# One long convolution in a two-block transformer kernel: running sums in a PSUM bank, three channel tiles for GpSimd

## The reference, cut to what matters

```python
def _mixer(x, mem, ...):
    h = _rmsnorm(x, norm_mix_g)
    proj = h @ w_in
    p_a, p_b, q, p_g = jnp.split(proj, IN_SPLITS, axis=-1)
    gb, gc, v = jnp.split(p_a, 3, axis=-1)
    y_a = (gb * _causal_dwconv(gc * v, conv_a_w)) @ w_a_out        # 3 taps
    u, ug = jnp.split(p_b, 2, axis=-1)
    u = u * jax.nn.sigmoid(ug)
    u = _causal_dwconv(u, conv_b_w) + conv_b_bias                  # 31 taps, per channel
    u = jax.nn.silu(_layernorm(u, ln_b_g, ln_b_b))
    y_b = u @ w_b_out
    k, vm = jnp.split(_rmsnorm(mem, norm_mem_g) @ w_kv, 2, axis=-1)
    ...                                                            # attention of q over k, vm
    g = jax.nn.sigmoid(p_g + b_gate)
    return (g[0] * y_a + g[1] * y_b + g[2] * y_c) @ w_o
```

## Time and profile before

| | |
|---|---|
| time, median of 3 runs | 1298.03 us (1295.3 to 1300.07) |
| the profiled execution's time | 1297.04 us |
| its span in the trace | 1294.9 us |
| TensorE busy | 1199.2 us, 93% of the span |
| VectorE busy | 877.6 us, 68% |
| GpSimd busy | 375.7 us, 29% |

### The profile page before, as it was taken

How to read it: one execution, slowest core, us unless ns; L and a number is a source line. 1 busy time by engine, 2 the same in 40 slices (tenths; PEclk the granted TensorE clock), 3 DMA queues, 4 the chain that set the end, 5 groups by cost and what they waited for, 6 DMA issues and landing times.

```text
span 1294.9 us, 20581 instructions
## 1 busy us (share of the span) xinstructions
PE 1199.2 (93%) x8047; PEld 1110.5 (86%) x8047; DVE 877.6 (68%) x1114; ACT 619.6 (48%) x824; POOL 375.7 (29%) x312
## 2 busy tenths in 40 slices
PE   4999889999899999999867889999999988999997
PEld 4999789999799899999766779999989777999996
DVE  3677998988466688888768846555565485555554
ACT  5554324344453454554657645444453474544442
POOL 1009999801300312222212414880010130100000
PEclk9999999999799999999978799999999979999999
DMA  8453445565226555554343028655555502555550
GB/s 268 162 179 131 146 139 183 165 195 190 70 98 189 164 183 176 190 193 164 113 139 130 1 66 235 195 195 184 179 164 190 193 1 71 188 180 182 193 192 35
DMA packets 139427, 201.01 MB, mean 155 GB/s; under 512 B 3252, under 2 KB 119988, under 8 KB 139372
## 3 DMA queue, kind: packets, MB, share of 16 engines
q1 hardware_dynamic: 138128, 195.83, 46.1%
q0 software_dynamic: 912, 3.17, 1.0%
q10 hardware_dynamic: 332, 1.25, 0.3%
HBM read 199.20 MB, written 1.05 MB: 155 GB/s over the span
## 4 chain that ended last, share of the span: by engine, by line
PE 76%; DVE 16%; ACT 5%; issue 2%; POOL 1%; DMA 1%; POOLq 0%; ACTq 0%; SPq 0%; DVEq 0%
PE ps L1456 70%; DVE wlo L896 4%; DVE work L1039 4%; PE ps L1555 4%; ACT whi L511 2%; PE ps L1591 1%; DVE work L996 1%; DVE work L1091 1%; ACT p_hi L531 1%; DMA x<-in_x 1%; POOL q_lo L395 1%; DVE stat L986 1%; DVE work L1206 0%; DVE stat L983 0%; DVE misc L976 0%
## 5 line engine op out<-in xcount | busy, mean ns | idle before, releaser
L896 DVE TENSOR_TENSOR wlo<-raw,whi 128x2048 fp32r<-128x2048 f32 x174 | 405.4, 2333 | 216.4 <-ACT whi L511 216.3
L511 ACT ACTIVATE whi<-raw 128x2048 fp32r<-128x2048 f32 x189 | 361.0, 1915 | 277.3 <-PE ps L1456 272.2
L1456 PE MATMUL ps<-p_hi,whi 128*128 128x256 f32 x1632 | 466.5, 286 | 23.3 <-DVE wlo L896 18.6
L1456 PE MATMUL ps<-p_lo,whi 128*128 128x256 f32 x1632 | 464.9, 285 | 0.0
L1456 PE MATMUL ps<-p_hi,wlo 128*128 128x256 f32 x1632 | 464.7, 285 | 0.0
L1456 PEld LDWEIGHTS ps<-p_hi,whi 128*128 128x128 f32 x1632 | 316.2, 194 | 28.2 <-DVE wlo L896 12.4
L1456 PEld LDWEIGHTS ps<-p_lo,whi 128*128 128x128 f32 x1632 | 316.4, 194 | 1.5
L1456 PEld LDWEIGHTS ps<-p_hi,wlo 128*128 128x128 f32 x1632 | 316.3, 194 | 0.0
L1456 PE MATMUL ps<-whi,q_hi 128*128 128x512 f32 x376 | 147.3, 392 | 3.5 <-DVE wlo L896 2.0
L401 POOL TENSOR_TENSOR wlo<-raw,whi 128x2048 fp32r<-128x2048 f32 x15 | 69.5, 4637 | 276.9 <-ACT whi L511 276.9
L1456 PE MATMUL ps<-whi,q_lo 128*128 128x512 f32 x376 | 146.8, 390 | 0.0
(11 more groups left out here) (229 smaller groups left out, 1672.7 us busy)
## 6 DMA issues: line engine op xcount, KB each, us to landing
raw<-in_w_in SPq DMA_DIRECT2D x36, 1024.0 KB, 5.0
raw<-in_w_up SPq DMA_DIRECT2D x22, 1024.0 KB, 5.1
raw<-in_up_a SPq DMA_DIRECT2D x16, 1024.0 KB, 5.5
raw<-in_down_a SPq DMA_DIRECT2D x16, 1024.0 KB, 4.9
raw<-in_up_b SPq DMA_DIRECT2D x16, 1024.0 KB, 5.4
raw<-in_down_b SPq DMA_DIRECT2D x16, 1024.0 KB, 4.9
raw<-in_od_w_qkv SPq DMA_DIRECT2D x12, 1024.0 KB, 5.2
raw<-in_w_down SPq DMA_DIRECT2D x11, 1024.0 KB, 5.0
```

What stands on the lines that cost most here:

```text
L511: nc.scalar.activation(whi[:, g % R, :], raw[:, g % R, :], ACT.Copy).then_inc(hi_ready, 1)
L896: nc.vector.tensor_tensor(wlo[:, g % R, :], raw[:, g % R, :], whi[:, g % R, :].bitcast(F32), ALU.subtract).then_inc(lo_ready[g % R], 1)
L1456: ins = nc.tensor.matmul(dst, lhs, rhs, start=first and n == 0, stop=last and n == 2)
```

## The change

- The running sums of the long convolution on VectorE are the two halves of PSUM bank 7. The taps read `misc` and the weights in `vec` where they lie, so the copies are gone. The last odd tap writes into `conv`, and the last addition reads the even sum from the bank and this one from `conv`.
- GpSimd takes tiles 0, 2 and 4 in place of 6 and 7, and its product buffers are the first 512 columns of `work`; it no longer waits for `norm_tr`, only for the tile's input. VectorE takes tiles 1 (ugq), 3 and 5 (kv), 6 (cvb) and 7 (gate, one part a round).
- Keys use banks 0, 1, 2 and 0 again, values banks 3 to 6; bank 7 belongs to the sums. The attention's `prob` moves from column 0 of `work` to column 512.

```diff
-CONV_DVE = 6
+CONV_POOL = (0, 2, 4)
+CONV_DVE = (1, 3, 5, 6, 7)
...
-        prob = work[:, 0:1536].rearrange("p (b t n) -> p b t n", b=3, t=T)
+        prob = work[:, 512:2048].rearrange("p (b t n) -> p b t n", b=3, t=T)
...
-            pool.wait_ge(norm_tr, 8)
             steps = taps = 0
-            for c in range(CONV_DVE, KD):
+            for c in CONV_POOL:
                 pool.wait_ge(glu, 2 + c // 2)
...
-                        tap = xn[:, 0, S * (k % 2):S * (k % 2) + S]
+                        tap = work[:, S * (k % 2):S * (k % 2) + S]
...
-            acc = [work[:, 320:576], work[:, 576:832]]
-            TAPS = K_B + 3
+            acc = [bank(7, 0, S), bank(7, S, 2 * S)]
+            TAPS = K_B + 1
+            def conv_part(n, part):
+                c, base = CONV_DVE[n], TAPS * n
                 if part == 0:
-                    dve.wait_ge(glu, glu_at)
-                    nc.vector.tensor_copy(work[:, 0:UP], misc[:, bass.ds(c * UP, UP)]).then_inc(conv_tap, 1)
-                    nc.vector.tensor_copy(work[:, UP:UP + K_B], vec[:, bass.ds(c * NV + V_CONVB, K_B)])\
-                        .then_inc(conv_tap, 1)
-                    dve.wait_ge(conv_tap, base + 2)
+                    dve.wait_ge(glu, 2 + c // 2)
                 for k in (range(0, 8), range(8, 16), range(16, 24), range(24, K_B))[part]:
-                    src, w = work[:, k:k + S], work[:, UP + k:UP + k + 1]
+                    src, w = misc[:, c * UP + k:c * UP + k + S], gain(V_CONVB + k, c)
...
-                        dve.wait_ge(conv_tap, base + k + 1)
-                        nc.vector.scalar_tensor_tensor(out=acc[k % 2], in0=src, scalar=w, in1=acc[k % 2],
+                        dve.wait_ge(conv_tap, base + k - 1)
+                        dst = conv[:, c * S:(c + 1) * S] if k == K_B - 2 else acc[k % 2]
+                        nc.vector.scalar_tensor_tensor(out=dst, in0=src, scalar=w, in1=acc[k % 2],
                                                        op0=ALU.mult, op1=ALU.add).then_inc(conv_tap, 1)
...
             for i in range(4):
-                    free(i, USES["kv"][i])
-                    to_channels(G_KV + i, i, q_pair, 0, "n_mem" if i == 0 else None)
+                    free(i % 3, USES["kv"][i % 3] + i // 3)
+                    to_channels(G_KV + i, i % 3, q_pair, 0, "n_mem" if i == 0 else None)
+                free(3, USES["kv"][3])
                 for i in range(4):
-                    to_rows(G_KV + 4 + i, 2, q_pair, 2 * i, 4, 2, BW, i == 0, i == 3)
+                    to_rows(G_KV + 4 + i, 2, q_pair, 2 * i, 3, 2, BW, i == 0, i == 3)
```

More of the change, by code:

```diff
@@ L73 @@
     ("setup", {0: 1}), ("n_mix", LOW4), ("ugq", {1: 4, 2: 4}), ("setup2", {3: 1}), ("n_mem", LOW4),
-    ("kv", {**LOW4, **HIGH4}), ("cvb", {0: 4, 1: 4, 2: 4}), ("gate", {0: 4, 1: 4, 2: 4}),
+    ("kv", {0: 2, 1: 1, 2: 1, 3: 1, 4: 1, 5: 1, 6: 1}), ("cvb", {0: 4, 1: 4, 2: 4}), ("gate", {0: 4, 1: 4, 2: 4}),
     ("a_out", LOW4), ("att1", {2: 2, 3: 2, **HIGH4}), ("att_out", LOW4), ("b_out", LOW4),
@@ L644, in _ @@
                 act.wait_ge(slot_used, G_KV + i + 1)
-                nc.scalar.activation(kreg[:, BW * i:BW * (i + 1)], bank(i), ACT.Copy).then_inc(bank_read[i], 1)
+                nc.scalar.activation(kreg[:, BW * i:BW * (i + 1)], bank(i % 3), ACT.Copy).then_inc(bank_read[i % 3], 1)
                 hi(G_KV + i + 3)
@@ L650, in _ @@
                     for b in range(4):
-                        nc.scalar.activation(v_tok[:, b // 2, BW * (b % 2):BW * (b % 2) + BW], bank(4 + b),
-                                             ACT.Copy).then_inc(bank_read[4 + b], 1)
+                        nc.scalar.activation(v_tok[:, b // 2, BW * (b % 2):BW * (b % 2) + BW], bank(3 + b),
+                                             ACT.Copy).then_inc(bank_read[3 + b], 1)
                 hi(G_KV + 7 + i)
@@ L1020, in _ @@
             lo(2)
-            acc = [work[:, 320:576], work[:, 576:832]]
-            TAPS = K_B + 3
-            def conv_part(c, base, part, glu_at):
+            acc = [bank(7, 0, S), bank(7, S, 2 * S)]
+            TAPS = K_B + 1
+            def conv_part(n, part):
+                c, base = CONV_DVE[n], TAPS * n
                 if part == 0:
-                    dve.wait_ge(glu, glu_at)
-                    nc.vector.tensor_copy(work[:, 0:UP], misc[:, bass.ds(c * UP, UP)]).then_inc(conv_tap, 1)
-                    nc.vector.tensor_copy(work[:, UP:UP + K_B], vec[:, bass.ds(c * NV + V_CONVB, K_B)])\
-                        .then_inc(conv_tap, 1)
-                    dve.wait_ge(conv_tap, base + 2)
+                    dve.wait_ge(glu, 2 + c // 2)
                 for k in (range(0, 8), range(8, 16), range(16, 24), range(24, K_B))[part]:
-                    src, w = work[:, k:k + S], work[:, UP + k:UP + k + 1]
+                    src, w = misc[:, c * UP + k:c * UP + k + S], gain(V_CONVB + k, c)
                     if k < 2:
+                        if base and k == 0:
+                            dve.wait_ge(conv_tap, base)
                         nc.vector.tensor_scalar(acc[k], src, w, None, ALU.mult).then_inc(conv_tap, 1)
                     else:
-                        dve.wait_ge(conv_tap, base + k + 1)
-                        nc.vector.scalar_tensor_tensor(out=acc[k % 2], in0=src, scalar=w, in1=acc[k % 2],
+                        dve.wait_ge(conv_tap, base + k - 1)
+                        dst = conv[:, c * S:(c + 1) * S] if k == K_B - 2 else acc[k % 2]
+                        nc.vector.scalar_tensor_tensor(out=dst, in0=src, scalar=w, in1=acc[k % 2],
                                                        op0=ALU.mult, op1=ALU.add).then_inc(conv_tap, 1)
@@ L1043, in conv_part @@
                     nc.vector.scalar_tensor_tensor(
-                        out=conv[:, bass.ds(c * S, S)], in0=acc[0], scalar=vec[:, bass.ds(c * NV + V_CBIAS, 1)],
-                        in1=acc[1], op0=ALU.add, op1=ALU.add).then_inc(conv_tap, 1)
+                        out=conv[:, c * S:(c + 1) * S], in0=acc[0], scalar=gain(V_CBIAS, c),
+                        in1=conv[:, c * S:(c + 1) * S], op0=ALU.add, op1=ALU.add).then_inc(conv_tap, 1)
             def ugq(i, parts=()):
@@ L1054, in ugq @@
                 lo(G_UGQ + 4, i)
-                for part in parts[:1]:
-                    conv_part(0, 0, part, 2)
+                for n, part in parts[:1]:
+                    conv_part(n, part)
                 lo(G_UGQ + 5, i)
-                for part in parts[1:]:
-                    conv_part(0, 0, part, 2)
+                for n, part in parts[1:]:
+                    conv_part(n, part)
             ugq(0)
             normalise("n_mem", mem_rows)
-            ugq(1, (0, 1))
-            ugq(2, (2, 3))
+            ugq(1, ((0, 0), (0, 1)))
+            ugq(2, ((0, 2), (0, 3)))
             ugq(3)
@@ L1068, in _ @@
                 lo(G_KV + 3 + i)
-                conv_part(1 + i // 4, TAPS * (1 + i // 4), i % 4, 3)
+                conv_part(1 + i // 4, i % 4)
             gcv = work[:, 1344:1860].rearrange("p (b n) -> p b n", b=2)
@@ L1103, in _ @@
                 branch_a(i)
-                conv_part(3, 3 * TAPS, i, 3)
+                conv_part(3, i)
             for i in range(4):
@@ L1107, in _ @@
                     lo(G_GATE + 3 + j, i)
-                    if j:
-                        c = 4 + i // 2
-                        conv_part(c, c * TAPS, 2 * (i % 2) + j - 1, 4)
+                    if j == 1:
+                        conv_part(4, i)
             conv_t = conv.rearrange("p (c n) -> p c n", c=KD)
@@ L1673, in _ @@
                 to_channels(G_AO + i, i, q_pair)
-            pe.wait_ge(conv_tap, (K_B + 3) * CONV_DVE)
-            pe.wait_ge(pool_tap, K_B * (KD - CONV_DVE))
+            pe.wait_ge(conv_tap, (K_B + 1) * len(CONV_DVE))
+            pe.wait_ge(pool_tap, K_B * len(CONV_POOL))
             free(7, USES["att1"][7])
```

## The result

The changed kernel took 1276.39 us in the median of four runs (1273.66 to 1280.85), the one before 1299.05. These medians of four lie 22.7 us apart. The ratio of the two kernels is put at 0.985 (95% interval 0.982 to 0.988), which is 19.7 us. Two later comparisons gave the same 0.985 (0.981 to 0.990, and 0.982 to 0.989), with medians only 17.2 us apart each time. Over all runs the change takes 1278.3 us in the mean (14 runs) and the kernel before 1297.8 (34). So the gain is 19 to 20 us, where 17.6 were forecast, and the first pair of medians shows it 3 us too large.

A forecast was written before the change was run, and what follows sets the result against it. VectorE was taken to bound kv and cvb, TensorE what lies around them. The room's -17.9 us plus 0.3 in ugq gave -17.6: from 1297.04 to 1279.4, with the runs' median 1 us higher 1280.4; range 1276 to 1290.

The forecast's parts named there:

- The taps: VectorE's long convolution: with one SBUF and one PSUM tensor, taps take 0.40 us beside GpSimd instead of 0.60.
- a dearer tap: Rival, VectorE's taps: reading and writing PSUM makes each cost more, 1284.6 or some 1283.6 us in all; chance 0.14.
- reads and writes in turns: Rival, VectorE's taps: reads and writes of one bank alternate, another 0.267 us a tap, about 1304 us; chance 0.07.
- kv: Stage of eight VectorE parts from 108.14 us: 5.94 us each instead of 7.57, VectorE 1.6 us early, TensorE sets the pace.
- cvb: Stage of four VectorE rounds after kv: 17.77 us each instead of 19.41, group 35's `lo` done 1.4 us before TensorE wants it.
- The drift never reaches TensorE: In cvb, VectorE's rounds exceed TensorE's 17.34 us by 0.43 each, but TensorE never waits.
- one of the prediction's own signs of being wrong: In cvb: the prediction is wrong if TensorE waits for `lo` there.
- The room: Groups 13 to 34 on TensorE: unhindered, it starts group 35 at 232.9 instead of 250.79, so 17.9 us at most.
- ugq: Early stage where GpSimd now works beside VectorE: idle time covers its rounds, a later `lo` at the end costs +0.3 us.
- a late GpSimd: Rival, before att1's scores: GpSimd's convolution ends at 308, TensorE stands 10 us, 1290 us in all; chance 0.10.

The follow-up runs named there:

- the two SBUF and PSUM kernels: Kernel before with only the sums moved to PSUM, tiles and GpSimd's start as before: 1275.91 us; changed kernel with its sums in SBUF: 1293.76 us.
- the extra reductions: Changed kernel with three small extra VectorE reductions, results unused, in each cvb round: 1280.61 us median; group 12's end to first scores 200.7 us.
- the late start: Changed kernel with GpSimd waiting for the memory's transposes again (norm_tr 8) before its three tiles: 1310.02 us, ratio 1.010 to the kernel before.

## Why the prediction was right

**The taps** go at 0.39 us beside GpSimd, forecast 0.40, and the two SBUF and PSUM kernels show that the operand's memory is the cause. The rivals of a dearer tap and of reads and writes in turns are out: 477 ns against 479. (The second reckoned with 1.04 ns a column; 2.21 us for 2048 columns and 0.396 for 256 give 1.01, which changes nothing.) The Trainium skill (VectorE: DVE Perf Modes, the section on the TRN2 errata) gives a PSUM source 62 cycles more; for this instruction, with one of its two tensors in PSUM, the same two numbers show none of it.

**kv** came out better than forecast (5.5 us a part, not 5.94). A `lo` between free taps lost less to GpSimd: 2.36 us (140.99 to 143.35), not 2.77; only the first of the eight took 2.71. VectorE waits 2.13 us ahead of L1078, forecast 1.6.

**cvb** is the step that failed in its size. A round was forecast at 17.77 us, to leave 1.4 us at group 35. It takes 18.30:

```profile
192.00 0.68 DVE L1078 TENSOR_TENSOR work<-ps,work 128x512 f32<-128x512 f32 x1
...
194.81 1.31 DVE L1089 TENSOR_SCALAR work<-work,vec 128x256 f32<-128x256 f32 x2
...
200.53 0.68 DVE L1097 TENSOR_TENSOR work<-ps,work 128x512 f32<-128x512 f32 x1
...
207.17 3.22 DVE L1040 SCALAR_TENSOR_TENSOR ps<-misc,vec,ps 128x256 f32<-128x256 f32 x8
210.30 0.68 DVE L1078 TENSOR_TENSOR work<-ps,work 128x512 f32<-128x512 f32 x1
```

The taps did what they should (3.13 us). But the two products of the short convolution, L1089, take 1.23 us until the next instruction in all four rounds, where the forecast's round had had them in 0.66 (211.75 to 212.41 in the trace before). That round was the usual one there; the four took 0.52, 1.23, 0.66 and 0.66. The dear one, in the trace before:

```profile
191.77 1.30 DVE L1088 TENSOR_SCALAR work<-work,vec 128x256 f32<-128x256 f32 x2
193.00 2.37 DVE L1091 SCALAR_TENSOR_TENSOR work<-work,vec 128x256 f32<-128x256 f32 x4
```

Without GpSimd's convolution the two take 0.52 or 0.53 in every round, so the loss is GpSimd's doing. With the sums back in SBUF they took 0.53 to 0.68. In the change GpSimd stands at another point of its work when they come, and in its two further traces one round was cheaper, 17.7 us beside 18.3 for the one before it, because L1100 took 0.60 there and not 1.15. That is where their 0.6 us less in the piece come from. The step that failed is that the rest of a round was taken over at its old price (19.41 - 4.81) when the taps changed. At the dearest price of the old trace, 1.23, the same sum gives 18.34 a round and a group 35 that is 0.9 us late. The slack was nothing, as the extra reductions show, and the change stays 0.6 to 1.2 us above the floor. "The drift never reaches TensorE" was wrong by that much, and one of the prediction's own signs of being wrong came up: TensorE waited for `lo`, at group 32, where 1.1 us of slack had been forecast, and at group 35 (timeline of TensorE in the change):

```profile
213.23 0.38 PE L1456 MATMUL ps<-p_hi,whi 128*128 128x256 f32 x1 [0.40 <-DVE wlo L896]
...
231.08 0.39 PE L1456 MATMUL ps<-p_hi,whi 128*128 128x256 f32 x1 [0.32 <-DVE wlo L896]
```

**The room** was put at 17.9 us and is 19.9 (214.47 - 194.54). The term is the 22 groups at 5.78 us each. A value group has the same columns in half as many products of twice the width, and costs 5.44: ScalarE's `whi` instructions in kv, each started by the end of a value group, stand that far apart, in the kernel before already:

```profile
128.51 1.92 ACT L511 ACTIVATE whi<-raw 128x2048 fp32r<-128x2048 f32 x1 [3.12 <-PE ps L1456]
133.95 1.92 ACT L511 ACTIVATE whi<-raw 128x2048 fp32r<-128x2048 f32 x1 [3.52 <-PE ps L1456]
```

Four value groups are 4 x 0.34 = 1.4 us, and the rest is 5.76 against 5.78. So the number came out near by two misses that go against each other: the room was 2.0 us larger, cvb cost 0.6 to 1.2 us that were not forecast, and the 0.3 of ugq didn't come. From 17.6 that makes 18.7 to 19.3, what the piece shows.

**ugq** lost nothing: L1053, the former L1052, still waited 1.90 us for ScalarE (2.27 before), so VectorE came at most 0.4 us later there and not 1.7. The +0.3 at its end didn't come: 93.19 to 98.64, from ScalarE's last upper part to group 12, is 5.45 us against 94.17 to 99.65 before.

**GpSimd** ended at 283.2, forecast 285, and its first part of att1 started at 292.07, forecast 293.9:

```profile
280.28 2.87 POOL L448 TENSOR_TENSOR misc<-misc,work 128x256 f32<-128x256 f32 x1
292.07 2.36 POOL L396 TENSOR_TENSOR p_lo<-qreg,p_hi 128x512 fp32r<-128x512 f32 x1 [8.92 <-ACT p_hi L560]
```

It waited 8.92 us there; the rival of a late GpSimd is real, but needs the late start.

**What the prediction didn't ask** is which part of the change is needed. It costed five tiles and the early start as harmless, and that they are, but by its own sum it could have said that the sums alone bring everything.

## What to carry to other kernels

When VectorE and GpSimd slow each other, look for the second SBUF operand of VectorE's instruction: a running sum in a spare PSUM bank removed it at no cost per instruction, and all of the gain came from there. Work that is taken from an engine in a stage where it isn't on the chain brings nothing, and may need an early start elsewhere merely not to cost. The price of an instruction that meets another engine depends on where that engine stands at the time, and a change beside it can move that: reckon with its dearest occurrence as well as its usual one. Take a group's price from a group of the same shape.

## What the runs showed of the hardware

- VectorE's taps, beside GpSimd's products and additions, last 694 ns in the median with two tensors read from SBUF and 477 with one of them in PSUM. Where the result is written made no difference (472 ns into SBUF).
- A VectorE instruction that reads and writes the same PSUM bank (256 columns in, 256 out) lasts 477 ns, as one with all operands in SBUF and an idle GpSimd (479). No row of the kernel before could show this.
- TensorE's three passes over a 1 MB group took 5.44 us as 24 products of 512 columns and 5.76 us as 48 of 256.
- The same kernel's spans differ by over 7 us (1271.9 and 1279.3) with nearly the same work in kv, cvb and gate: group 12 (granted clock 1.00 or 0.57) and the stages from the first attention on (from 300 to 500 us 0.97 or 0.93) run at a changing granted clock. A change of 1 us is seen in a stretch of the trace, not in the time.
